# The last token tile of the output projection as four column groups of the array, and the expert bias rows added over four expert periods

## The reference, cut to what matters

```python
mix = group_norm_concat([attn, conv_out, cross], g_mix_out)   # widths 512, 256, 256
h = x + mix @ w_out                                           # 1024 x 1024
hn = rmsnorm(h, g_ffn_norm).reshape(B * T, D_MODEL)
y = h + moe(hn, w_router, b_router, w_gate_up, b_gate_up, w_down, b_down)
# moe: logits = hn @ w_router + b_router; top 4 of 32; gates = softmax of the four
#   h1 = xb @ w_gate_up[e] + b_gate_up[e]                     # 1024 x 2048
#   out = ((up + 1) * glu) @ w_down[e] + b_down[e]            # 1024 x 1024
#   sum over the four experts of gate * out
```

## Time and profile before

| what | value |
|---|---|
| median of three runs | 1507.87 us (1506.69 to 1511.36) |
| profiled execution | 1507.95 us, of which the span is 1506.1 us |
| PE busy | 1429.7 us, 95% of the span |
| DVE, ACT, POOL busy | 1200.6, 987.4, 278.7 us |
| DMA | 461.76 MB, 307 GB/s in the mean |
| granted PE clock | 0.979 of full speed in the mean |

### The profile page before, as it was taken

One profiled execution on the slowest core, in us unless ns is written; L12 is line 12 of the kernel. 1 busy time (PEld: TensorE's weight loads), 2 busy tenths in 40 slices (PEclk: granted clock), 3 DMA queues, 4 the chain that ended last, 5 costly groups with the idle time before them and its releaser, 6 DMA issues.

```text
span 1506.1 us, 18757 instructions
## 1 busy us (share of the span) xinstructions
PE 1429.7 (95%) x6713; PEld 1034.5 (69%) x6713; DVE 1200.6 (80%) x1111; ACT 987.4 (66%) x944; POOL 278.7 (19%) x183
## 2 busy tenths in 40 slices
PE   5999889877999999999999999999999999999994
PEld 3776555455777777777777777777777777777773
DVE  2434334475999999999999999999999999999995
ACT  2123331165777777777777777777777777777773
POOL 2001111133222111111111111111122112112212
PEclk9999989978999999999999999999999999999998
DMA  9611007258999999999999999999999999999973
GB/s 365 224 73 41 28 10 317 105 196 274 365 363 373 366 363 355 372 362 356 380 367 369 367 366 357 358 364 367 363 361 364 366 361 357 357 372 365 363 295 136
DMA packets 51575, 461.76 MB, mean 307 GB/s; under 512 B 10708, under 2 KB 14758, under 8 KB 25812
## 3 DMA queue, kind: packets, MB, share of 16 engines
q1 hardware_dynamic: 39460, 437.72, 75.8%
q0 software_dynamic: 10128, 20.40, 6.2%
q10 hardware_dynamic: 1936, 2.99, 0.8%
HBM read 447.78 MB, written 24.27 MB: 313 GB/s over the span
## 4 chain that ended last, share of the span: by engine, by line
PE 90%; DVE 3%; DMA 2%; issue 2%; ACT 2%; POOL 1%; POOLq 0%; SPq 0%; ACTq 0%; DVEq 0%
PE psum L1957 23%; PE psum L1959 23%; PE psum L1958 23%; PE psum L1623 6%; PE psum L1781 4%; PE psum L1970 2%; PE psum L1943 2%; PE psum L1952 2%; PE psum L1595 1%; DMA y_tbl<-area,row_i 1%; POOL ring L552 1%; DMA area<-in_x_prompt 1%; PE psum L1933 1%; PE psum L1692 0%; PE psum L1808 0%
## 5 line engine op out<-in xcount | busy, mean ns | idle before, releaser
L1471 DVE TENSOR_TENSOR low<-raw,high 128x2048 fp32r<-128x2048 f32 x384 | 869.6, 2285 | 36.6 <-ACT high L916 34.4
L916 ACT CAST high<-raw 128x2048 fp32r<-128x2048 f32 x384 | 724.8, 1913 | 98.1 <-PE psum L1959 98.0
L1957 PE MATMUL psum<-high,area_r 128*104 128x512 f32 x1536 | 613.4, 399 | 1.2 <-DVE area_r L1465 1.2
L1959 PE MATMUL psum<-low,area_r 128*104 128x512 f32 x1536 | 604.1, 393 | 0.0
L1958 PE MATMUL psum<-high,area_r 128*104 128x512 f32 x1536 | 603.1, 393 | 0.0
L1959 PEld LDWEIGHTS psum<-low,area_r 128*104 128x104 f32 x1536 | 258.1, 168 | 98.2
L1957 PEld LDWEIGHTS psum<-high,area_r 128*104 128x104 f32 x1536 | 258.6, 168 | 90.1 <-DVE area_r L1465 1.7
L1958 PEld LDWEIGHTS psum<-high,area_r 128*104 128x104 f32 x1536 | 258.8, 168 | 89.2
L615 POOL DMA_INDIRECT area<-hn_tbl,idx_i x33 | 94.4, 2861 | 311.5 <-DVE idx_i L1394 305.1
L599 POOL CAST pick_r<-area 64x104 fp32r (+1 forms) x33 | 30.3, 918 | 519.8 <-PE psum L1959 519.6
L1623 PE MATMUL psum<-ring 128*128 128x272 f32 x448 | 107.6, 398 | 1.2 <-DVE area L1108 0.9
(11 more groups left out here) (223 smaller groups left out, 905.2 us busy)
## 6 DMA issues: line engine op xcount, KB each, us to landing
raw<-in_w_gate_up SPq DMA_DIRECT2D x128, 2048.0 KB, 10.7
raw<-in_w_down SPq DMA_DIRECT2D x64, 2048.0 KB, 9.9
ring<-in_w_in SPq DMA_DIRECT2D x7, 1024.0 KB, 20.3
area<-in_w_out SPq DMA_DIRECT2D x1, 4096.0 KB, 18.7
ring<-in_w_mem_kv SPq DMA_DIRECT2D x1, 2048.0 KB, 11.4
area<-in_x_prompt SPq DMA_DIRECT2D x4, 512.0 KB, 12.1
ring<-in_mem_kT SPq DMA_DIRECT2D x1, 2048.0 KB, 8.5
ring<-in_cache_mem_v SPq DMA_DIRECT2D x1, 2048.0 KB, 8.2
```

What stands on the lines that cost most here:

```text
L916: nc.scalar.copy(high_w(i), raw_w(t)).then_inc(sem("w_high"), 1)
L1471: v.tensor_tensor(low_w(t), raw_w(t), high_w(i), ALU.subtract).then_inc(sem("w_low"), 1)
L1957: mm(bank, high, wh, start=start, stop=False)
L1959: return mm(bank, high, wl, start=False, stop=stop)
```

## The change

Tile 4 of the output projection is made as four groups of 32 columns of the array: group g multiplies slices 2g and 2g+1 and writes rows 32g to 32g+31 of one PSUM bank (`group_part`, one for each half of 512 columns). ACT copies the whole bank to `hrow` with the scale of each group's part, and one product with a 128 x 32 matrix of stacked identities adds the four groups (`group_sums`); DVE adds the input rows (`h_sums`). The input rows of tile 4 have a buffer of their own (`xr4`). The logits, the choice and the gates of tile 3 now come behind that, and chunk 4 of expert 0 is loaded one tile earlier.

The bias rows of tiles 0 and 1 stay in period 0; those of tiles 2, 3 and 4 move to periods 1, 2 and 3. POOL waits for the scatter of the period ahead of each, and each scatter for the bias DMA ahead of it.

```diff
--- before.py
+++ after.py
@@ -204 @@
 sqs = view(ring, W_OFF + 10240, [2, 3, P])
+xr4 = view(ring, W_OFF + 11008, [D])
+assert W_OFF + 12032 <= 30720
@@ -279 @@
-    return banks[((4, 5), (3, 7))[j % 2][half]]
+    return banks[((4, 5) if j == 0 else (3, 7))[half]]
...
-    return yrow[:, j % 2, :] if j < 4 else bias4
+    return yrow[:, 1, :] if j == 1 else bias4
@@ -318 @@
 RING = [("part", 0, 0), ("ss", 0, 0)] + [("part", 0, x) for x in range(1, 6)]
-for _j in range(1, NTT):
+for _j in range(1, NTT - 1):
     RING += [("ss", _j, 0)] + [("part", _j, x) for x in range(3)] + [("hT", _j - 1, 0), ("hT", _j - 1, 1), ("part", _j, 3),
                                                                   ("lg", _j - 1, 0), ("part", _j, 4), ("part", _j, 5)]
-RING += [("hT", NTT - 1, 0), ("hT", NTT - 1, 1), ("lg", NTT - 1, 0)]
+RING += [("ss", NTT - 1, 0), ("group", NTT - 1, 0), ("group", NTT - 1, 1), ("sum", NTT - 1, 0), ("sum", NTT - 1, 1)]
+for _j in (NTT - 2, NTT - 1):
+    RING += [("hT", _j, 0), ("hT", _j, 1), ("lg", _j, 0)]
 RING_AT = {job: i for i, job in enumerate(RING)}
@@ -335 @@
     return {"part": ("h_part", 6 * j + x + 1), "ss": ("ss3_ready", j + 1), "hT": ("hT_ready", 2 * j + x + 1),
-            "lg": ("lg_ready", j + 1)}[kind]
+            "lg": ("lg_ready", j + 1), "group": ("group_out", x + 1), "sum": ("h_part", 6 * (NTT - 1) + x + 1)}[kind]
@@ -425 @@
         src = x_prompt[0, j * P:(j + 1) * P, :] if j < 4 else x_sample.rearrange("b t d -> (b t) d")
-        sp.dma_start(xr[0:ROWS[j], j % 2, :], src).then_inc(sem(f"ld_xr{j % 2}"), 16)
+        dst = xr[0:ROWS[j], j % 2, :] if j < 4 else xr4[0:NSM]
+        sp.dma_start(dst, src).then_inc(sem("ld_xr4" if j == 4 else f"ld_xr{j % 2}"), 16)
...
     load_x(1)
+    load_x(4)
     sp.wait_ge(sem("ulr_ready"), 1)
@@ -440 @@
                 load_chunk(0, q)
-        if j == NTT - 1:
+        if j == NTT - 2:
             sp.wait_ge(sem("h_part"), 6 * j + 4)
             load_chunk(0, 4)
-        sp.wait_ge(sem("h_part"), 6 * (j + 1))
-        if j + 2 < NTT:
+        sp.wait_ge(sem("h_part"), 6 * (j + 1) if j < 4 else 26)
+        if j + 2 < 4:
             load_x(j + 2)
@@ -554 @@
         pool.wait_ge(sem("ss3_ready"), j + 1)
+        if j == NTT - 1:
+            nc.gpsimd.tensor_tensor(rs3[:, 12:13], ss3[:, 12:13], mh[:, 0:1], ALU.pow).then_inc(sem("rs3_ready"), 1)
+            return
         nc.gpsimd.tensor_tensor(rs3[0:n, 3 * j:3 * j + 3], ss3[0:n, 3 * j:3 * j + 3], mh[0:n, 0:3], ALU.pow).then_inc(sem("rs3_ready"), 1)
@@ -567 @@
     for j in range(1, NTT):
-        mix_scale(j)
+        if j < NTT - 1:
+            mix_scale(j)
+        if j == NTT - 2:
+            mix_scale(NTT - 1)
         h_scale(j)
@@ -581 @@
-    pool.wait_ge(sem("h_pe"), 6 * NTT)
+    pool.wait_ge(sem("group_pe"), 2)
     nc.gpsimd.memset(gate3, 0.0).then_inc(sem("gate3_zero"), 1)
@@ -620 @@
         pool.wait_ge(sem("yrow_ready"), n * 2)
+        if isinstance(n, int) and 0 < n <= 3:
+            for j in ((0, 1) if n == 1 else (n,)):
+                pool.wait_ge(sem(f"bias_added{j}"), 16)
         wait(pool, "scattered", n * 16 - 16)
@@ -639 @@
             pick_rows(n + 2, k)
+            if isinstance(n, int) and 0 < n < UB:
+                pool.wait_ge(sem("scattered"), n * 16)
+                add_bias(n + 1)
             gather(n + 2, k + 2)
@@ -656 @@
             bias_row(j)[0:ROWS[j], :], None,
-            bounds_check=bound, oob_is_err=False, compute_op=ALU.add).then_inc(sem(f"bias_added{j if j == 4 else j % 2}"), 16)
+            bounds_check=bound, oob_is_err=False, compute_op=ALU.add).then_inc(sem(f"bias_added{j}"), 16)
...
     pool.wait_ge(sem("row_ready"), 1)
-    for j in range(NTT):
-        add_bias(j)
-    period(0, 0)
-    for par, times in ((0, 2), (1, 2), (4, 1)):
-        pool.wait_ge(sem(f"bias_added{par}"), 16 * times)
-    for u in range(1, UB):
+    add_bias(0)
+    add_bias(1)
+    for u in range(UB):
         period(u, u)
+    pool.wait_ge(sem("bias_added4"), 16)
     with pool.Fori(1, NE // UB - 1) as it:
@@ -821 @@
         n = ROWS[j]
-        ac.wait_ge(sem("h_part"), 6 * (j + 1))
+        ac.wait_ge(sem("h_part"), 6 * (j + 1) if j < 4 else 26)
         wait(ac, f"st_hn{j % 2}", 16 * (j // 2))
@@ -898 @@
     mix_squares(3)
-    for j in range(2, NTT):
+    for j in range(2, NTT - 1):
         h_T(j - 1)
...
             mix_squares(4)
-        if j == NTT - 1:
-            gate_exp(0, NTT - 1, P)
         h_square(j)
+    ac.wait_ge(sem("rs3_ready"), NTT)
+    ac.wait_ge(sem("st_h0"), 32)
+    for half in range(2):
+        ac.wait_ge(sem("group_pe"), half + 1)
+        nc.scalar.activation(hrow[:, 0, half * 512:(half + 1) * 512], ring_bank("group", NTT - 1, half)[:, :],
+                             ACT.Copy, scale=rs3[:, 12:13]).then_inc(sem("group_out"), 1)
+    h_T(NTT - 2)
+    h_square(NTT - 1)
+    gate_exp(0, NTT - 1, P)
     h_T(NTT - 1)
@@ -918 @@
         ac.wait_ge(sem("w_used"), used)
-        if isinstance(n, int) and n == 1:
-            for par, times in ((0, 2), (1, 2), (4, 1)):
-                ac.wait_ge(sem(f"bias_added{par}"), 16 * times)
+        if isinstance(n, int) and n == 2:
+            ac.wait_ge(sem("bias_added1"), 16)
         wait(ac, "scattered", n * 16 - 32)
@@ -975 @@
                 high_part(n, i + 3, last)
-            if isinstance(n, int) and n == 0 and i in (0, 1, 3, 4, 5):
-                bias_evict((0, 1, 3, 4, 5).index(i))
+            if isinstance(n, int) and n < UB and (i == 1 or i == 0 == n):
+                bias_evict(n + i)
             if last and i == 6:
@@ -1008 @@
         n = ROWS[j]
-        if j in (2, 3):
-            ac.wait_ge(sem(f"bias_added{j % 2}"), 16)
+        if j >= 2:
+            ac.wait_ge(sem(f"bias_added{0 if j == 2 else j - 1}"), 16)
         for half in range(2):
@@ -1209 @@
         ss = ring_bank("ss", j, 0)
+        if j == NTT - 1:
+            v.tensor_scalar(ss3[0:64, 12:13], ss[0:64, 0:1], 1.0 / 512, EPS, ALU.mult, ALU.add)
+            v.tensor_scalar(ss3[64:P, 12:13], ss[64:P, 0:1], 1.0 / 256, EPS, ALU.mult, ALU.add).then_inc(sem("ss3_ready"), 1)
+            return
         for c, width in ((0, 512), (1, 256), (2, 256)):
@@ -1228 @@
                 in1=xr[0:n, par, cols] if x % 3 == 0 else hrow[0:n, par, cols], op0=ALU.mult, op1=ALU.add).then_inc(sem("h_part"), 1)
+
+    def h_sums():
+
+        dv.wait_ge(sem("ld_xr4"), 16)
+        for half in range(2):
+            cols = slice(half * 512, (half + 1) * 512)
+            dv.wait_ge(sem("sum_pe"), half + 1)
+            v.tensor_tensor(hrow[0:NSM, 0, cols], ring_bank("sum", NTT - 1, half)[0:NSM, :], xr4[0:NSM, cols], ALU.add).then_inc(sem("h_part"), 1)
@@ -1359 @@
-    for j in range(1, NTT):
+    for j in range(1, NTT - 1):
         mix_means(j)
         h_parts(j, (0, 1, 2))
-        if j + 1 < NTT:
-            square_sums(j + 1)
+        square_sums(j + 1)
         h_parts(j, (3,))
...
         choose(j - 1)
-        if j == NTT - 1:
-            gates(0, NTT - 1, P, 1)
         h_parts(j, (4, 5))
+        if j == NTT - 2:
+            mix_means(NTT - 1)
         h_norm(j)
+    h_sums()
+    logits(NTT - 2)
+    choose(NTT - 2)
+    h_norm(NTT - 1)
+    gates(0, NTT - 1, P, 1)
     places(0, NTT - 1, P)
@@ -1790 @@
+    def group_squares():
+
+        pe.wait_ge(sem("sq_sums"), NTT)
+        bank = ring("ss", NTT - 1, 0)
+        for g, c in enumerate((0, 0, 1, 2)):
+            last = mm(bank[g * NSM:(g + 1) * NSM, 0:1], sqs[:, 0, c, 0:NSM], c_("ones")[:, 0:1], start=True, stop=True)
+        last.then_inc(sem("sq_pe"), 1)
+
+    def group_part(half):
+
+        bank = ring("group", NTT - 1, half)
+        for t in range(2):
+            for g in range(4):
+                last = mm(bank[g * NSM:(g + 1) * NSM, :], zT[:, 2 * g + t, NPR:NT], wo[:, 2 * g + t, half * 512:(half + 1) * 512],
+                          start=(t == 0), stop=(t == 1))
+        last.then_inc(sem("group_pe"), 1)
+
+    def group_sums():
+
+        for half in range(2):
+            bank = ring("sum", NTT - 1, half)
+            pe.wait_ge(sem("group_out"), half + 1)
+            mm(bank[0:NSM, :], c_("eye2"), hrow[:, 0, half * 512:(half + 1) * 512], start=True, stop=True).then_inc(sem("sum_pe"), 1)
+
     def router_rows(j):
@@ -1918 @@
         part(j, 5)
+    group_squares()
+    group_part(0)
+    group_part(1)
+    places(NTT - 3)
+    group_sums()
+    router_rows(NTT - 2)
+    router(NTT - 2)
     places(NTT - 2)
@@ -2003 @@
         pe.wait_ge(sem("gate3T_ready"), 1)
-        if j >= 2:
-            pe.wait_ge(sem("bias_row"), 2 * j - 2)
         for half in range(2):
@@ -2019 @@
-        first = isinstance(n, int) and n == 0
-        if first:
+        early = n if isinstance(n, int) and n < UB else None
+        if early == 0:
             bias_term(0)
-            bias_term(1)
+        if early is not None:
+            bias_term(early + 1)
         gate_up(n, 0, last, k)
...
         gate_up(n, 2, last, k)
```

(10 more changed lines are left out.)

## The result

The changed kernel takes 1485.4 us (median of 4 runs, 1484.61 to 1486.74) against 1507.33 us of the kernel before beside it. The ratio is 0.9844, 95% interval 0.9823 to 0.9866: faster by 1.6%. The forecast was 1486.2. The profiled execution took 1486.74 us, its span is 1485.0 us, 21.1 less than before.

The account below looks back on a forecast made before the run. PE bounds every steady period, so only losses ahead of the loop or in its first period can be regained: 1507.95 less 7.8 (last token tile) less 13.9 (bias rows) gives 1486.2 us, range 1483.5 to 1489.

Parts of the forecast that it names:

- Step 2: Tile 4's products on PE: the 32 records of four groups run at once in 3.7 us, bounds 3.4 and 14.3.
- groups in turn: Rival: tile 4's groups don't run side by side and take 14.3 us; total 1496.8 us, chance 0.05.
- Steps 3 to 5: ACT copies banks, 0.69 us each; PE and DVE add; PE transposes tile 3 from 283.1, its choice done 4.9 us later.
- R: The moment PE starts to transpose tile 3, forecast at 283.1 us from the start of the span.
- Step 6: Tile 4 on DVE: h_norm 2.06 us, gates 1.82, places with slots 1.80; its logits start at 293.7.
- PE stood at clock 0.50 there and will again.: From tile 4's logits to the loop's first product: unchanged and simply earlier, PE again at clock 0.50.
- Gain of A: Front part with the new last token tile: tile 4's logits start 7.8 us earlier, bounds 5.8 and 9.
- Part B: Bias rows: first bias product to x_rows in period 0 takes 18.7 us, 15.3 less; after moved products return, gain 13.9.
- The added waits: POOL's and scatters' waits around the moved bias DMAs, and ACT's wait for a bias DMA: hidden, costing nothing.
- with 3 us to spare: ACT's `bias_evict(3)` in period 2: 19 us of cover for a bias DMA that took 6.2 to 16.4 us.
- the queues give it back: Rival: bias DMAs build a backlog of some 6 us in periods 0 to 3 that reaches PE; 1490.5 us, chance 0.13.

Follow-up runs that it names:

- e7: The changed kernel with POOL's memset moved behind the gates of tiles 0 to 3, beside DVE's places and slots: 1490.81 us.
- e10: The changed kernel plus idle products in six of PE's gaps before the first x_rows (3, 1, 3, 1, 8 and 2): 1483.74 us, ratio 0.9825.
- e1: The kernel before plus only the groups and new order of the front part, all five bias tiles still in period 0: 1501.65 us, ratio 0.9965.
- e2: The kernel before plus only the bias tiles spread over four periods, the front part as before: 1492.94 us, ratio 0.9916.
- e3: The changed kernel without the products, copies and DMAs of bias tiles 2, 3 and 4: median 1488.05 us.
- e6: The changed kernel plus a POOL copy of 512 rows between DRAM tables behind each of the three moved bias adds: 1497.83 us.
- e11: The changed kernel plus idle products only in the last two gaps before the first x_rows (8 and 2): 1484.68 us, ratio 0.9826.

## Why the prediction was right

The forecast of 1486.2 us met 1485.4, and its range held. Step by step:

*Step 2, the groups.* 3.62 us against 3.7 forecast, within the bounds of 3.4 and 14.3. The estimate from the Trainium skill ("TensorE: Matmul & The Clock Gate", section "Measured speedup vs the span model"), its 79% for three tiles taken over to four, was 4.5. The trace does not bear it out: four tiles are 3.95 times faster than in turn (14.3 / 3.62), 99% of four. The side-by-side row was the better guide (its 3.8 times are 95% of four, not 96). The rival "groups in turn" is out, and two positions (7.06 us) show its mechanism at half size.

*Steps 3 to 5.* R came 5.98 us behind M, forecast 6.1. From R to the end of the choice 4.79 against 4.9. ACT's copies took 0.69 and were hidden as told.

*Step 6.* h_norm 1.99 against 2.06, gates 1.89 against 1.82. Places with slots were mis-sized: 1.09 us against 1.80. The duration came from the trace before, where 0.63 of it lay beside POOL's memset. In both kernels POOL issues its memsets right behind `h_scale(4)` (297.06 before, 288.57 after). Before, DVE's places and slots come next behind `h_norm(4)`; in the changed kernel the gates stand between, and the memset (289.64 to 291.43) lies beside them and is over when the slots start. In e7, which holds the memset back to the slots, the time is lost again. The prediction had the new order of DVE and didn't ask what the memset lay beside. From M to the logits of tile 4: 24.50 us before, 15.74 after, 8.76 gained where I had 7.8.

*"PE stood at clock 0.50 there and will again."* This is the sentence of step 6 that failed. PE did stand at 0.50, but for longer: twelve products of gate_up instead of six, 0.20 us each. From the first product of the loop to the first bias product it took 8.84 us instead of 7.54, 1.30 lost. That it can be avoided is shown by e10. The windows tell where it comes from. The stretch at half clock, before:

```profile
297.20:317.60 20.40, 9.99 (x53) 7.94 (x54) 15.61 (x34) 11.02 (x14) 6.78 (x7) 0.50 0.33 106
```

After:

```profile
288.20:312.00 23.80, 13.97 (x63) 10.76 (x64) 18.26 (x43) 11.22 (x15) 6.92 (x7) 0.50 0.31 108
```

In e7:

```profile
291.30:315.10 23.80, 12.17 (x59) 9.62 (x60) 19.31 (x42) 11.19 (x15) 6.99 (x7) 0.50 0.31 107
```

From 317.8, 312.1 and 315.2 on the clock is 1.00. It came back 40.7 us behind M before and 34.5 after, 6.2 earlier; the first product of the loop stood 37.8 behind M before and 28.7 after, 9.1 earlier. So nearly 6 us of the head are slow instead of nearly 3, and the 2.9 us between, at 0.43 us a product where it could be 0.23, are the 1.3 lost. In e7 the clock came back 34.5 behind M too, but its head starts 1.8 us later than in the changed kernel, and that is the four slow products fewer, 8 instead of 12. B alone has 6; every kernel with A's front order and without idle products has more (8 in e7, 10 to 12 in the others). What sets the moment at which the clock comes back is open.

*Gain of A.* 8.76, plus 0.31 between the logits and the head, less 1.30: 7.77 against a forecast of 7.8. Two terms of about a microsecond each were wrong and cancelled; that the sum fits to a tenth is luck. Taken alone (e1), A gave 7.38, with half a microsecond lost in a longer stalled period 0.

*Part B.* First bias product to x_rows 18.83 us against 18.7; gain 15.22 against 15.3; 1.28 returned in periods 1 to 3 against 1.4; in sum 13.94 against 13.9. e2 shows 13.67 for it alone.

*The added waits.* Hidden, as said, but not "with 3 us to spare". ACT came to `bias_evict(3)` 18.4 us after the DMA's issue (394.29 - 375.85; forecast 19), and that DMA needed 17.8 us, where I had taken before's 16.4 as the longest. The cover was 0.7 us. What lies behind it, the 6 us until PE needs the copy (gate_up 4 at 400.72), is the real margin. Why the DMAs land later is not shown. They do in every kernel whose period 0 no longer stalls: the DMA of tile 0 took 10.9 and 11.0 us in the kernel before and in e1, and 12.5 to 14.8 in the others; that of tile 1 took 16.4 in both, and 18.0 to 20.3 in the others. The scatters' waits of 4.1 and 3.2 us cost nothing, as said.

*The rival "the queues give it back"* had the right places (gather and chunks) and a wrong size. I priced a bias DMA at 3.6 us of 16 engines from a share and the free time at 1.4 us from a share of 0.96. But a share counts the time in which packets are under way, and this rises without more being moved: 0.96 at 362 GB/s before, 1.00 at 360 after. Counted in bytes, and as an estimate, the bias rows need 0.52 MB where 0.8 MB were free. So there is no backlog that reaches PE (e3 shows 1.32 us for products and queues together), where I had 6 us of it. Nor do the 6 us follow from the two terms: two bias DMAs in period 0 and one each in periods 1 and 2, at 3.6 us each against 1.4 free in a period, make some 10, more than the slack of 8. That slack was not tested by the bias rows; by the estimate above, e6 shows 1.75 us lost of a backlog of some 9 us at the second dose, and of some 14 at the third 7.6 us, of which 1.6 are the clock, so a slack of 8 us is about right.

*The rest*, 0.61 us, is M itself, 277.59 instead of 276.98: the front part of that execution. 21.71 - 0.61 is the 21.1 of the spans.

## What to carry to other kernels

Where a loop is bound by one engine in every period, a change ahead of it is worth what the steady periods start earlier, and it can be summed from the timeline in steps of a microsecond; but ask of each duration taken from the old trace what ran beside it there, and whether the change moves that too. When products use a quarter of the array's columns, put four of them at four column positions (the two orders that ran took the same time) and add the results with one more product. If the first products of a loop come behind waits, look at their distance, and don't count on the clock coming back earlier with them (9.1 us earlier brought it back 6.2 earlier here): small idle products in the gaps, no longer than the gaps, gave 2.7 us here, and too many of them took it back.

## What the runs showed of the hardware that I had not expected

- Products of 32 columns at four column positions take a quarter of the time (3.62 of 14.3 us) also with 512 columns each, whether neighbours in the order share a position or not (3.67); at two positions they take half (7.06).
- A DVE `tensor_scalar` of 128x128 f32 from SBUF to SBUF takes 0.23 us alone and, beside a memset of POOL, lasts until 0.08 us behind the memset's end (0.86 and 1.72 us). The `scalar_tensor_tensor` ahead of it, which reads PSUM, kept its 0.28 us.
- A DMA share near 1 doesn't tell what the queues can still take: 1.00 stood beside 360 GB/s and 1.02 beside 392.
- An accumulating DMA of 128 rows landed after 6.2 to 16.4 us in the kernel before, whose period 0 stalls, and after 14.8 to 20.3 in the changed kernel; the same two DMAs of period 0 took 10.9 and 16.4 us before and 14.8 and 20.3 after.
- The three moved bias adds held POOL for 6.30, 6.30 and 6.06 us in the middle of the expert loop, against 1.36 to 2.67 in period 0, before and after. The cause is open; it cost nothing here.
- The granted clock can rise and fall again before a loop begins: in e11 the transposes at 306.68 took 0.93 us and the products from 309.38 on were at 0.43 us again.
- With the front order of part A the clock came back 34.5 us behind M, both in the changed kernel and in e7, whose loop starts 1.8 us later; before, it came back 40.7 behind M.
